# Ten of twelve modulation parts turned into columns by DMAs through DRAM instead of by TensorE

## The reference

```python
def _modulation(cvec, ada_w, ada_b):
    m = jax.nn.silu(cvec) @ ada_w + ada_b
    return jnp.split(m[:, None, :], 6, axis=-1)
...
    for l in range(DEPTH):
        sh1p, sc1p, g1p, sh2p, sc2p, g2p = _modulation(c_ctx[None, :], ada_w[l], ada_b[l])
        sh1s, sc1s, g1s, sh2s, sc2s, g2s = _modulation(c, ada_w[l], ada_b[l])
        hp = _rmsnorm(xp, norm1_w[l]) * (1 + sc1p) + sh1p
        hs = _rmsnorm(xs, norm1_w[l]) * (1 + sc1s) + sh1s
        ...  # mixer of the layer: op, os_
        xp = xp + g1p * op
        xs = xs + g1s * os_
        ...  # norm, sc2, sh2, experts, g2
```

## Time and profile before

| | |
|---|---|
| time, median of 3 runs (lowest to highest) | 1755.2 us (1754.45 to 1755.74) |
| span of the profiled execution, first to last instruction | 1752.8 us |
| instructions | 30448 |
| TensorE matmul busy | 1607.8 us, 92% |
| VectorE busy | 518.0 us, 30% |
| ScalarE busy | 698.3 us, 41% |
| DMA from and to HBM | 291 GB/s over the span |
| mean granted clock of TensorE | 0.962 |

### The profile page before, as it was taken

How to read it: one execution, slowest core, us unless ns; L and a number is a source line. 1 busy time by engine, 2 the same in 40 slices (tenths; PEclk the granted TensorE clock), 3 DMA queues, 4 the chain that set the end, 5 groups by cost and what they waited for, 6 DMA issues and landing times.

```text
span 1752.8 us, 30448 instructions
## 1 busy us (share of the span) xinstructions
PE 1607.8 (92%) x13039; PEld 1131.2 (65%) x13039; DVE 518.0 (30%) x857; ACT 698.3 (40%) x1055; POOL 18.6 (1%) x25
## 2 busy tenths in 40 slices
PE   5999999989999999999997998999999999999995
PEld 3767766856666666666665776866666666666663
DVE  1034044151222223232323216232222223232324
ACT  2213322233454545454544204225454545454444
POOL 0000000010000000000000000010000000000000
PEclk8999888989999999999998999899999999999998
DMA  9967566546999999999998333438999999999970
GB/s 315 323 227 266 193 251 240 204 168 272 354 370 357 366 358 365 359 358 367 354 370 301 87 118 156 186 126 320 356 368 359 354 365 363 364 358 366 353 286 25
DMA packets 130113, 510.50 MB, mean 291 GB/s; under 512 B 11257, under 2 KB 19601, under 8 KB 97297
## 3 DMA queue, kind: packets, MB, share of 16 engines
q1 hardware_dynamic: 124832, 506.23, 75.9%
q10 hardware_dynamic: 5232, 3.57, 0.7%
HBM read 506.64 MB, written 3.15 MB: 291 GB/s over the span
## 4 chain that ended last, share of the span: by engine, by line
PE 58%; ACT 23%; DVE 12%; issue 5%; DMA 1%; DVEq 1%; ACTq 0%
PE psum L1230 57%; ACT arena L503 22%; DVE arena L1121 8%; DVE arena L1032 1%; PE psum L1551 1%; DMA arena<-in_moe_router_bias 1%; DVE arena L803 0%; DVE arena L1126 0%; ACT arena L526 0%; DVE arena L845 0%; ACTq L500 0%; DVEq L1134 0%; ACT arena L744 0%; ACT L514 0%; PE psum L1698 0%
## 5 line engine op out<-in xcount | busy, mean ns | idle before, releaser
L1230 PE MATMUL psum<-arena 128*64 128x256 f32 (+9 forms) x12756 | 1577.3, 348 | 112.9 <-DVE arena L1032 63.7
L1230 PEld LDWEIGHTS psum<-arena 128*64 128x64 f32 (+3 forms) x12756 | 1100.9, 136 | 582.4 <-issue 347.1
L503 ACT ACTIVATE arena<-psum 128x512 f32<-128x512 f32 (+4 forms) x514 | 455.7, 903 | 573.8 <-PE psum L1230 468.0
L1121 DVE TENSOR_TENSOR arena<-psum,arena 128x512 f32<-128x512 f32 x128 | 137.7, 1076 | 523.8 <-ACT arena L503 523.8
L503 ACT ACTIVATE arena<-arena 128x512 bf16<-128x512 f32 (+1 forms) x144 | 88.6, 625 | 148.8 <-DVE arena L1121 146.2
L1126 DVE TENSOR_TENSOR arena<-arena 128x512 bf16<-128x512 f32 x128 | 88.7, 693 | 101.1 <-ACT arena L503 101.1
L1105 DVE COPY arena<-psum 128x512 f32<-128x512 f32 x64 | 44.3, 693 | 182.4 <-PE psum L1230 182.4
L825 DVE TENSOR_TENSOR arena<-psum,arena 128x16 f32<-128x16 f32 x12 | 2.1, 175 | 144.4 <-PE psum L1230 144.4
L510 ACT ACTIVATE arena<-arena 128x512 f32<-128x512 f32 x20 | 12.3, 629 | 73.6 <-DVE arena L845 73.6
L845 DVE SCALAR_TENSOR_TENSOR arena<-psum,arena 128x128 f32<-128x128 f32 x64 | 17.8, 343 | 65.6 <-PE psum L1230 65.6
L676 ACT ACTIVATE arena<-psum 128x256 f32<-128x256 f32 x64 | 24.7, 386 | 30.0 <-PE psum L1230 30.0
(11 more groups left out here) (137 smaller groups left out, 309.6 us busy)
## 6 DMA issues: line engine op xcount, KB each, us to landing
arena<-in_moe_w_gate SPq DMA_DIRECT2D x64, 2048.0 KB, 7.9
arena<-in_moe_w_up SPq DMA_DIRECT2D x64, 2048.0 KB, 12.6
arena<-in_moe_w_down SPq DMA_DIRECT2D x64, 2048.0 KB, 9.3
arena<-in_ada_w SPq DMA_DIRECT2D x24, 2048.0 KB, 15.1
arena<-in_hgrn_w_in SPq DMA_DIRECT2D x10, 2048.0 KB, 13.5
arena<-in_na_w_qkv SPq DMA_DIRECT2D x6, 2048.0 KB, 18.1
arena<-in_hgrn_w_out SPq DMA_DIRECT2D x1, 4096.0 KB, 12.6
arena<-in_na_w_o SPq DMA_DIRECT2D x1, 4096.0 KB, 13.7
```

The costliest lines, as they stand in the source:

```text
L503: return act.activation(out, in_, ACT.Copy, **kw)
L1121: dve.tensor_tensor(y_rest[:, :, ps].rearrange("s k p -> s p k"), psum[:, 6 + half, :].rearrange("s (p k) -> s p k", k=K), y[:, j, 0, :, p ...
L1230: return pe.matmul(out, lhsT, rhs, start=start, stop=stop, skip_group_check=True, **kw)
```

## The change

For parts 2 to 11 the turning leaves TensorE. GpSimd waits for the copy of a row, stores it with two DMAs (one for each group, 4 partitions x 512 numbers) to a scratch tensor in DRAM, waits for both, and loads it back with one DMA of 64 partitions x 8 x 8: the row of 512 becomes 64 partitions of 8 features, for each of four partial sums and two groups, in pieces of 8 numbers. `modulation(p)` waits for the loads of both rows, sums the four partial sums with a reduction, and adds the bias as before. The buffers for it lie where the rank table of the experts stands later. `ada(n)` for n from 5 on waits for the copy of the row before instead of, every second time, for `modulation`; the copy of row n from 6 on waits until row n - 2 is stored, since it uses the same half of `mrow`.

```diff
+        ada_cols = cut(2 * 8 * K, (2, 8, K), at=rank_at)
+        ada_sum = cut(2 * K, (2, K), at=rank_at + 2 * 8 * K)
+        ada_rows_out = nc.dram_tensor("ada_rows", (2, 2, 4, 2, BLOCK), F32).ap()
...
@@ gpsimd
+            for n in range(4, 24):
+                part, half = n // 2, n % 2
+                row = ada_rows_out[part % 2, half]
+                pool.wait_ge(ada_row, n + 1)
+                if part >= 4:
+                    pool.wait_ge(mod_done, part - 1)
+                for s in range(2):
+                    pool.dma_start(row[:, s], mrow[s:s + 97:32, half * BLOCK:(half + 1) * BLOCK]).then_inc(ada_stored, 16)
+                pool.wait_ge(ada_stored, 32 * (n - 3))
+                ps = slice(half * (P // 2), (half + 1) * (P // 2))
+                pool.dma_start(ada_cols[ps, part % 2], row.rearrange("g s (p k) -> p (g s) k", k=K)).then_inc(ada_cols_in, 16)
@@ scalar, ada_rows(n)
-                if n % 2 == 0 and n >= 2:
+                if n in (2, 4):
                     act.wait_ge(sel_ps, n // 2)
+                elif n >= 6:
+                    act.wait_ge(ada_stored, 32 * (n - 5))
@@ vector, modulation(n)
-                dve.wait_ge(sel_ps, n + 1)
-                dve.tensor_tensor(mod[:, l, j], psum[:, 7, 0:2 * K].rearrange("p (k s) -> p k s", s=2),
+                if n < 2:
+                    dve.wait_ge(sel_ps, n + 1)
+                    columns = psum[:, 7, 0:2 * K].rearrange("p (k s) -> p k s", s=2)
+                else:
+                    dve.wait_ge(ada_cols_in, 32 * (n - 1))
+                    dve.wait_ge(mod_done, n)
+                    link(dve.tensor_reduce(ada_sum.rearrange("p s k -> p (s k)"),
+                                           ada_cols[:, n % 2].rearrange("p (g s) k -> p (s k) g", g=4), AX.X, ALU.add))
+                    columns = ada_sum.rearrange("p s k -> p k s")
+                dve.tensor_tensor(mod[:, l, j], columns,
@@ tensor, ada(n)
-                if n % 2:
+                if n in (2, 4):
+                    pe.wait_ge(mod_done, n // 2)
+                elif n:
                     pe.wait_ge(ada_row, n)
-                elif n:
-                    pe.wait_ge(mod_done, n // 2)
@@ tensor, midway()
-                    if part is not None:
-                        ada_columns(part)
```

More of the change, by code:

```diff
@@ L113, in build @@
         router_b = cut(2 * E, (2, E))
+        rank_at = top[0]
         rank = cut(2 * E, (2, E))
@@ L227, in build @@
         ada_ps, ada_row, sel_ps, mod_done = sem("ada_in_psum"), sem("ada_rows"), sem("ada_cols_in_psum"), sem("mod_done")
+        ada_stored, ada_cols_in = sem("ada_rows_stored"), sem("ada_cols_in")
         sq_done, ssum, root = sem("squares"), sem("square_sums"), sem("root")
```

## The result

The kernel before took 1754.97 us in this comparison (median of 4 runs), the changed one 1740.16 (1737.8 to 1743.2, 4 runs): ratio 0.9917, 95% interval 0.9903 to 0.9931. It is 14.8 us faster, where 35 were forecast; the time lies in the range, above the likeliest case's own (1711 to 1738). The profiled execution has a span of 1736.0 us (1752.8 before).

The account below looks back on a forecast made before the run. TensorE, busy 92% of the span with its clock below full, was taken as the bound. Removal 47.4 less losses 8.3, tail 1.3 and clock 2 gave 35.8 us gained, so 1720 us; range 1702 to 1766.

Parts of the forecast that it names:

- the likeliest case: T near 9 and 11 us, time 1711 to 1738 us, forecast 1720, chance 0.45.
- The removal: Taking 2-column matmuls off TensorE in projections 2 to 9: 29.9 us of columns plus 17.5 of clock, 47.4 us gained.
- clock part: Half-clock falls during or just behind the 2-column matmuls in projections 2 to 9 would go: 17.5 us gained.
- The limits: Longest T before VectorE's queue delays later work: 8.6, 10.9, 8.3, 8.2, 13 and 8.7 us for parts 2, 3, 4, 7, 8, 9.
- T: Time from the end of a row's copy to its part's sum on VectorE: 9.0 us alone, 11.3 for a pair.
- store leg: GpSimd's two stores of a row to DRAM, until their semaphore: taken as 4.0 us.
- load leg: GpSimd's load of a row back from DRAM, 512 pieces of 32 bytes: taken as 5.0 us.
- losses: Time given back in the mixer's projections where T passes what VectorE's order allows: 8.3 us in sum.
- the tail: From row 21 to VectorE's copy of the mixer's output, ahead of the output projection: T - 7.7, a loss of 1.3 us.
- The second failure: Clock falling in TensorE's new waits of 2 to 3 us: 2 us lost, bounds 0 to 6.
- The slower one: Rival: VectorE's in-order queue waits behind the DRAM trip; legs of 7.9 us give 1783 us, 28 slower; chance 0.14.
- break-even: Each leg of the DRAM trip at about 6.5 us costs 48 us, all that was won.

Follow-up runs that it names:

- both stored first: Changed kernel, with GpSimd issuing the stores of both rows of a part before it waits and loads both: 1734.78 us, ratio 0.9898 to the kernel before.
- ScalarE stores: Changed kernel, with ScalarE issuing a row's two stores behind its copy and GpSimd only loading: 1734.80 us, ratio 0.9889 to the kernel before.
- stored twice: Changed kernel, with GpSimd storing each row twice, one after the other, before it loads: 1776.43 us, ratio 1.0139 to the kernel before.
- Light loads: Changed kernel, mixer weight blocks from the sixth on loading only one eighth: 2273.74 us with other router choices, so read only up to row 21.

## Why the prediction was off

**The removal was right.** 47.4 us forecast, 47.6 measured in the stretch; its clock part 17.5 against 16.4. By difference the columns made some 31 where 29.9 stood: the total comes closer than its two parts do, and that much is luck. The clock was the second largest term, and it was read from the half-clock windows and the slower second halves, not from TensorE's busy share.

**The limits and the way the loss is made were right.** With the measured T the prediction's own limits give what T has over them as losses, and to that the half clock is added (half of TensorE's busy time in such stretches). The last column is the kernel's stretch less 182.9 us:

```
kernel              T over its limit, parts 2 3 4 7 8 9     sum   clock  together  measured
changed             4.0 + 0.9 + 6.2 + 7.8 + 0 + 7.5         26.4   10.4    36.8      35.5
both stored first   4.2 + 0   + 5.6 + 6.3 + 0 + 5.0         21.1    9.2    30.3      29.0
ScalarE stores      3.7 + 0   + 5.2 + 4.4 + 0 + 5.1         18.4   10.2    28.6      29.1
stored twice        6.5 + 4.9 + 7.6 + 20.1 + 0.9 + 15.4     55.4   13.1    68.5      69.1
```

**The step that failed is the size of T, and in it the store leg.** "I take 4.0 us for the store leg ... and 5.0 for the load leg ... nearer the lower one for the smaller sizes." In the six parts the store leg was 5.8 to 8.0 us (6.4 for row 5, 6.7 and 6.9 for rows 18 and 19), and in a pair it counts twice, as the second row stands behind the first one's. The load leg was 6.0 for part 2, but 2.4 to 4.9 in the pairs, under the forecast 5.0. T was 12.6 alone where 9.0 stood, and 14.5 to 16.2 in the three pairs that cost most, where 10.3 to 11.3 stood. Of the bounds, the 7.9 us of a 256 KB store beside loads was the near one for the store leg: of two properties of that row, its size and what it ran beside, I scaled by the size. Light loads show that the other weighs more: an 8 KB store drops from 5.5 to 1.9 us with them, a 256 KB one from 9.7 to 2.3. The text even says that rows come just as three blocks are asked for. The losses were 26.4 in place of 8.3. The profiled span gained 16.8 us in place of 35.8: of the 19.0 that lack, T makes 18.1 and the clock (below) 8.4; the tail gives 4.1 back and the earlier start 2.0. That makes 20.4, so 1.4 us too much are accounted for.

The Trainium skill's figure for such a DMA ("DMA: Bandwidth & Descriptors", Anatomy of one DMA — SWDGE (gpsimd) path: about 2.0 us fixed, plus the bytes over 436 GB/s) is near the 1.7 and 2.4 us measured while the engines were almost idle, and far from the 5.5 and 5.8 beside weights; the forecast's 4.0 and 5.0 lay between the two.

**The second failure is the clock.** "I take 2 us in all for it, 0 to 6 as bounds"; it was 10.4. That estimate rested on one wait of 2.1 us which the clock survived; the four long waits that came were 4.4 to 8.3 us. The first failure made the second larger: at the forecast T, the waits would have stayed under 3 us. That the clock would then have held is not shown: where ScalarE stores, a wait of 3.0 us (160.5 to 163.5) came with half clock from 162.7 to 169.6.

**The tail** went as its formula has it: T was 5.4 for part 10, since the DMA engines are idle there, and T - 7.7 = -2.3; it gained 2.8 us. Forecast was a loss of 1.3, with T taken as in the loaded stretch.

**The rivals.** The slower one names the right mechanism; its break-even, legs of 6.5 us, was passed by part 9's store legs (6.7 and 6.9) and not reached by its load leg (4.3), and the run that stores twice is slower than before. What it lacked is that most late loads get short.

## What to carry to other kernels

Here a small DMA took its time mainly from the loads that it ran beside, so bound one by the nearest row beside the same load, and only then by size. A wait put into an in-order queue costs what it has over the slack of all that stands behind it: put its consumer as late as the data allows (here one round, worth 36 us) before shortening the trip, which brought some 5, at the edge of what the intervals tell apart. And look for the clock in both directions: taking out matmuls with few columns gave it back, and it fell again where TensorE came to wait.

## What the runs showed of the hardware

- Sixteen 2-column matmuls per part hold TensorE busy and yet cost the clock (0.50 in ten stretches): with 256 columns in their place the ten falls go (1.00 from 50 to 337 us), and the kernel is 18.6 us faster.
- An 8 KB store on GpSimd's queue lands in 1.7 us with almost idle DMA engines, in 1.9 beside light loads and in 5.5 beside the full weight loads. There ScalarE's queue is no faster (legs of 6.4 and 6.2 us).
- A load that comes after a burst of weight loads is short: the median was 5.8 us in the changed kernel and 2.4 where the trips came late. One that ran beside a 4 MB block just asked for still took 6.8.
